# A hybrid encoder layer on eight cores: half of the transposes of the joint projection block moved to DMA, with shifts of loads, gate sums and one multiply

## The chip, the cores and the metric

The kernel runs as one program on all 8 cores of one Trainium2 chip. Each core works on its own rows, and no core talks to another. The metric is the device time in microseconds (us) of the slowest core. Engines are named as the profile names them: PE is TensorE (PEld its weight loads), DVE is VectorE, ACT is ScalarE, POOL is GpSimd, SP is SyncE, which here only issues DMAs.

## The reference, cut to what matters

One layer over sequences of 1024 channels:

```
h   = rmsnorm(x) * (1 + scale) + shift          # scale, shift, gate from silu(c) @ w_ada
z   = h @ w_in                                  # split: a, ga, u, v, gb, ma, mb
y_a = (real 2-D FFT of a, then a map per group) * silu(ga)
y_b = u * (w_s @ layernorm(v) + b_s) * silu(gb) # inside chunks of 128 positions
out = (sigmoid(ma) * (y_a @ w_pa) + sigmoid(mb) * (y_b @ w_pb)) @ w_out
y   = rmsnorm(x + gate * out) * final_g
```

Sizes: 16 prompts of 2048 positions and 4 samples of 4096 positions. Each core gets 6144 positions, as three units of 2048. The first unit is one sequence; the other two are either the two halves of a sample or two more prompts, and the kernel treats them together, as the "joint" pair.

## The kernel before, in words

Every engine runs one list of instructions in order, and so does the DMA queue of SP. The order is written out by hand: a class keeps, for each engine, the list and the semaphore waits that reads and writes of named 512-byte pieces of memory call for. A wait stands in front of its instruction, and all that is behind it on that engine waits too. All DMAs issued by SP go to one queue.

The work of a core falls in these stretches:

- The **first projection block** (an `ABlock` with f = 1, called `A`) computes the column section "a" of the first unit, chunk by chunk of 128 positions, does the first step of the FFT with one matmul (`stage1`), and writes the result to DRAM (`Gd`).
- Tiles 0 and 1 of 512 positions are done as a pair. `v_section`, `silu_section` and `u_section` are projections, with the second FFT step (`s3_single`) between them. `channel_tables` then builds tables from small inputs that `late_tabs` loads: cosines, biases, and, in the same group of DMAs and under the same semaphore, `final_g`. After it come `sgu`, `ga_section` with the last step of the FFT (`z_tr`, `fourier_gate`), then `merge_gates` and `merge` for eight blocks (`dmc`), and `out_chunk`.
- Tiles T = 2 and 3 run in the main loop. Beside their own work they sum up the gate vectors of the other units: `gate_load` brings rows of w_ada, `gate_acc` adds them on DVE.
- The **joint projection block** (`ABlock` with f = 0, called `A2`) comes after tile 3: 8 groups of 4 chunks for units 1 and 2. Chunks of x are loaded by SP into a ring of six slots. `sq` squares a pair of chunks on ACT, `rstd` makes 1/rms on POOL, `sc` scales the pair on DVE and then lets SP load into the freed slots. `fe` turns a group of four scaled chunks from positions by channels to channels by positions: 32 PE transposes into four PSUM banks, then eight moves out of PSUM that also apply scale and shift, four on DVE (line 473) and four on ACT (line 478). `a_proj` is 8 matmuls and a move on DVE (line 313); `stage1` is one matmul, a move, and a write to `Gd` (line 516). Group q + 1 is transposed between chunk 1 and chunk 2 of group q.
- Tiles 4 to 11 run in the main loop again. The input of tiles 3 and 5 to 11 is transposed by DMA (`dma_t`, line 439), and scale and shift are applied in place on DVE (`modulate`, line 445). At tiles 4 and 8 a new unit begins: w_out is loaded again by POOL's own DMA queue (`w_out_load`, line 689) and each of its eight rows of blocks is multiplied by the gate on POOL (`gate_mul`, line 694), between the additions that POOL does for `merge` (line 822).

`sgu` (line 755) makes four heads. For each head DVE writes one of two small buffers (line 761), and POOL multiplies it into the result (line 766). `fourier_gate` (lines 788 and 793, DVE) uses the memory of the first of these two buffers too, so it waits for POOL.

`out_chunk` (line 620) has two halves of 8 matmuls. With `split`, the first six of the first half are issued before the wait for the last blocks of the merge.

Of the kernel before, what the change touches and what calls it, by code (L numbers as in the profile page):

```python
# [11 lines left out]
D = 1024  # L12
# [198 lines left out]
def build_nc():  # L211
# [72 lines left out]
    semnames = (["pe", "act", "dve", "pool", "s_tab", "s_tb2", "s_id", "s_wst", "s_e", "s_gr", "s_gb", "s_wpa", "s_wpb", "s_wout"]  # L284
# [72 lines left out]

    def late_tabs():
# [7 lines left out]
        tab(fg_bc, dram_ap(final_g, 0, [[0, 128], [1, D]]))  # L366
        S.dma("sp", tabs, "s_tb2", writes=["tab2"] + ck)
# [74 lines left out]
    def modulate(off, slot):  # L442
        hT = hview(off)
        for kc in range(8):
# [8 lines left out]
    def fe_t(xoff):  # L453

        xr = bv(xoff, 4096).rearrange("p (j d) -> p j d", j=4)
        banks = []
        for kp in range(4):
# [8 lines left out]
    def fe_e(banks, off, slot):  # L466
        hT = hview(off)
        for kp, b in enumerate(banks):
            for kk in range(2):
                kc = 2 * kp + kk  # L470
                hk = gk(off + 1024 * kc, 1024)
                if kp % 2 == 0:
# [140 lines left out]
    def out_chunk(tb, T, j, k, split=False):  # L613
# [3 lines left out]
        xv = fv(XS[k], 1024)  # L617
        for half in range(2):
            b = newbank()
            mm = [lambda e, b=b, dmc=dmc, half=half: e.matmul(  # L620
                ps[b][:], lhsT=tb.mg[:, dmc, j * 128:(j + 1) * 128], rhs=w_out_sb[:, dmc, half * 512:(half + 1) * 512],
                start=(dmc == 0), stop=(dmc == 7)) for dmc in range(8)]
            cut = 6 if split and half == 0 else 0
            if cut:
                S.pe(mm[:cut], reads=gk(tb.m, 1024 * cut) + woutk, writes=[("ps", b)])
            S.pe(mm[cut:], reads=gk(tb.m, 8192) + woutk, writes=[("ps", b)])
# [10 lines left out]
        def fin():  # L637
            S.op("dve", lambda e: e.scalar_tensor_tensor(out=xv, in0=xv, scalar=stat[:, 1, si:si + 1], in1=fg_bc,
                                                         op0=ALU.mult, op1=ALU.mult),
                 reads=xk + [("st1", si), "tab2"], writes=xk)  # L640
# [111 lines left out]
    def sgu(tb):  # L752
        for h in range(4):
# [12 lines left out]
            S.op("pool", lambda e, h=h, ty=ty: e.tensor_tensor(out=tb.sgb[:, h, :], in0=ty, in1=tb.sgb[:, h, :], op=ALU.mult),  # L766
                 reads=gk(to, 1024) + sk, writes=sk)
# [58 lines left out]
    class ABlock:  # L826
# [3 lines left out]
        def __init__(self, f, nq, ring, N1, src, dst, xoffs, extra=()):  # L830
# [139 lines left out]
    pair = (T0, TB1)  # L970
    s3_begin(1)
# [3 lines left out]
    late_tabs()  # L975
# [11 lines left out]
    w_out_load()  # L987
    gate_load(0, 0)
# [54 lines left out]
    for T in range(2, NT):  # L1043
# [9 lines left out]
        def after(sec):  # L1053
# [7 lines left out]
            if T == 3 and sec < 3:  # L1061
                for kc, k in (((), ((0, 4), (1, 5), (2, 6)), ((3, 4), (4, 5), (5, 6)))[sec]):
                    gate_acc(2, kc, k, 7)
                for kc, k in ((((0, 4), (1, 5), (2, 6)), ((3, 4), (4, 5), (5, 6)), ((6, 4), (7, 5)))[sec]):
                    gate_load(kc, k)
                if sec == 2:
                    gate_bias(1, 6)
# [4 lines left out]
            if t == 0 and sec == 2:  # L1072
                gate_fetch(u)
                w_out_load()
# [3 lines left out]
        silu_section(tb, SEC["GB"], tb.sgb, tb.b, (lambda fc: s3j(fc - 1) if fc else None) if T == 4 else None)  # L1078
# [5 lines left out]
        sgu(tb)  # L1084
        ga_section(tb, u, t, (lambda fc: z_tr(0, fc)) if T == 4 else (lambda fc: z_tr(1, fc)) if T == 5 else None)
# [12 lines left out]
        for dmc in range(8):  # L1098
# [49 lines left out]
        elif isA:  # L1148
            A2.fe(0)
            A2.sq(3)  # L1150
# [6 lines left out]
        else:  # L1157
# [140 lines left out]
```

How the kernel before makes its waits and increments, by code:

```python
        def run(stream, e):  # L1176
            for it in stream:
                if it[0] == "wait":
                    e.wait_ge(sems[it[1]], it[2])
                elif it[0] == "raw":
                    it[1](e)
                else:
                    ins = it[1](e)
                    ins.then_inc(sems[it[2]], it[3])
```

## Time and profile before

| | us |
|---|---|
| runs | 1268.95, 1274.08, 1460.27 (median 1274.08) |
| profiled execution | 1266.18 |
| its span, slowest core (core 3) | 1264.6 |
| spans of all cores | 1256.6 to 1264.6 |
| PE busy | 1204.5 (95%) |
| DVE busy | 686.2 (54%) |
| ACT busy | 474.1 (37%) |
| POOL busy | 343.1 (27%) |
| mean DMA rate | 132 GB/s |

A row of a timeline gives the start and the length of a merged piece of work in us, the engine, the line of the kernel, the operation, the tiles, and the number of instructions. In square brackets stands the idle time of the engine before it and what ended it. SPq, POOLq and so on are the sequencers: a row SPq DMA_DIRECT2D is a DMA being issued, not moved. "DMA to landing" is the time from the issue until the data have landed. A window's row has the busy time and number of instructions of each engine, the granted clock of PE as a share of full speed, the busy share of the 16 DMA engines, and their rate.

### The profile page before, as it was taken

To read this page: it belongs to the slowest core of one execution; us is meant where nothing else is said; L and a number is where in the kernel's file an instruction comes from. 1 tells how busy PE (TensorE), PEld (TensorE's weight loads), DVE (VectorE), ACT (ScalarE), POOL (GpSimd) and SP (SyncE) were. 2 spreads that over 40 slices of the span, in tenths; PEclk is the share of its full clock that TensorE was granted. 3 is DMA by queue.
4 is the path that set the end of the run, shared out by engine and by line. 5 is a ranking of instruction groups with operands and counts; after the bars stand their busy time and mean duration, and the time that the engine had idled before them with its cause. 6 is when DMAs were issued, how large, how long until landed. Compare 5 with 4: busy or idle time off the path is not lost.

```text
span 1264.6 us, 19720 instructions; the slowest of 8 cores (1256.6 to 1264.6 us)
## 1 busy us (share of the span) xinstructions
PE 1204.5 (95%) x6128; PEld 563.5 (45%) x6128; DVE 686.2 (54%) x1109; ACT 474.1 (37%) x818; POOL 343.1 (27%) x430
## 2 busy tenths in 40 slices
PE   5799789999999899989999999999999999999997
PEld 1355444444444355545444444444444444444443
DVE  0483475465666568848356355545545654554444
ACT  1574232333323268835333332333242323332322
POOL 0231223631222232201811312313226323132211
PEclk9999899999999899999999999999999999999999
DMA  8999795334466278847230431513336415024121
GB/s 276 286 243 185 164 162 138 84 102 165 130 155 183 68 256 268 263 147 168 66 102 17 126 92 67 134 51 100 84 89 146 117 48 151 36 84 116 51 84 67
DMA packets 91124, 166.60 MB, mean 132 GB/s; under 512 B 39818, under 2 KB 52490, under 8 KB 89870
## 3 DMA queue, kind: packets, MB, share of 16 engines
q1 hardware_dynamic: 80606, 138.98, 36.9%
q0 software_dynamic: 9120, 17.96, 9.6%
q10 hardware_dynamic: 1296, 8.40, 2.0%
q8 instruction: 52, 0.85, 0.3%
q14 instruction: 50, 0.41, 0.1%
HBM read 143.41 MB, written 31.47 MB: 138 GB/s over the span
## 4 chain that ended last, share of the span: by engine, by line
PE 76%; DMA 7%; DVE 7%; issue 3%; POOL 2%; SPq 2%; ACT 1%; DVEq 0%; ACTq 0%; POOLq 0%
PE ps L699 35%; PE ps L620 12%; PE ps L503 6%; PE ps L811 6%; PE ps L817 6%; PE ps L709 5%; DMA arena<-w_ada 4%; PE ps L460 2%; POOL arena L766 2%; DVE arena L793 2%; DMA arena<-w_out 2%; DVE arena L788 1%; PE ps L924 1%; SPq L536 1%; DMA arena<-final_g 1%
## 5 line engine op out<-in xcount | busy, mean ns | idle before, releaser
L699 PE MATMUL ps<-arena 128*128 128x512 bf16 x2688 | 605.2, 381 | 3.7 <-DVE arena L761 2.4
L699 PEld LDWEIGHTS ps<-arena 128*128 128x128 bf16 x2688 | 262.8, 98 | 318.6 <-issue 10.9
L803 ACT ACTIVATE arena<-ps 128x512 bf16<-128x512 f32 x192 | 111.6, 595 | 244.1 <-PE ps L699 212.3
L822 POOL TENSOR_TENSOR arena<-arena 128x512 bf16<-128x512 bf16 x84 | 111.1, 1323 | 293.7 <-DVE arena L820 292.4
L620 PE MATMUL ps<-arena 128*128 128x512 bf16 x768 | 172.7, 379 | 4.4 <-DVE arena L822 3.0
L814 DVE TENSOR_TENSOR arena<-ps,arena 128x512 bf16<-128x512 f32 x96 | 66.2, 690 | 188.8 <-PE ps L811 182.9
L406 POOL TENSOR_TENSOR stat<-stat,eps_sb 128x1 f32<-128x1 f32 (+1 forms) x114 | 27.6, 242 | 396.4 <-ACT arena L632 291.7
L632 ACT ACTIVATE arena<-arena 128x1024 bf16<-128x1024 f32 x48 | 50.8, 1058 | 218.9 <-DVE arena L628 218.7
L419 ACT ACTIVATE arena<-arena 128x1024 bf16<-128x1024 f32 x96 | 101.4, 1056 | 73.8 <-DMA arena<-xB 54.0
L425 DVE TENSOR_SCALAR arena<-arena,stat 128x1024 bf16<-128x1024 f32 x96 | 84.5, 906 | 65.5 <-POOL stat L408 65.0
L620 PEld LDWEIGHTS ps<-arena 128*128 128x128 bf16 x768 | 74.2, 98 | 97.5 <-issue 10.1
L811 PE MATMUL ps<-arena 128*128 128x512 bf16 x384 | 99.4, 381 | 7.3 <-DVE arena L793 7.3
L313 DVE CAST arena<-ps 128x512 bf16<-128x512 f32 (+2 forms) x150 | 81.4, 583 | 43.3 <-ACT arena L311 19.2
L628 DVE TENSOR_TENSOR arena<-ps,arena 128x512 f32<-128x512 f32 x96 | 64.8, 688 | 71.1 <-PE ps L620 68.2
L817 PE MATMUL ps<-arena 128*128 128x512 bf16 x384 | 99.4, 382 | 0.0
L503 PE MATMUL ps<-arena 128*128 128x512 bf16 x384 | 91.8, 383 | 3.8 <-ACT arena L478 3.8
L709 PE MATMUL ps<-arena 128*128 128x512 bf16 x384 | 84.7, 379 | 0.0
L727 ACT ACTIVATE arena<-ps 128x512 bf16<-128x512 f32 x96 | 54.1, 600 | 64.7 <-PE ps L699 60.6
L408 POOL TENSOR_TENSOR stat<-stat,mh_sb 128x1 f32<-128x1 f32 (+1 forms) x114 | 71.2, 625 | 17.9 <-POOL stat L406 2.4
L820 DVE TENSOR_TENSOR arena<-ps,arena 128x512 bf16<-128x512 f32 x96 | 66.2, 690 | 15.0 <-PE ps L817 11.9
L720 ACT ACTIVATE arena<-ps,bnag 128x512 bf16<-128x512 f32 x48 | 33.4, 778 | 90.1 <-DVE bnag L716 90.1
L311 ACT ACTIVATE arena<-ps 128x352 bf16<-128x352 f32 (+3 forms) x103 | 44.9, 488 | 54.2 <-PE ps L924 15.8
(75 smaller groups left out, 942.2 us busy)
## 6 DMA issues: line engine op xcount, KB each, us to landing
arena<-xB SPq DMA_DIRECT2D x96, 512.0 KB, 5.2
arena<-xA SPq DMA_DIRECT2D x48, 512.0 KB, 6.3
yu<-arena SPq DMA_DIRECT2D x48, 512.0 KB, 2.8
arena<-w_ada SPq DMA_DIRECT2D x24, 512.0 KB, 6.0
arena<-w_in POOLq DMA_DIRECT2D x9, 1024.0 KB, 17.6
arena<-w_ada ACTq DMA_DIRECT2D x8, 1024.0 KB, 24.0
Gd<-arena SPq DMA_DIRECT2D x48, 128.0 KB, 4.7
arena<-Gd SPq DMA_DIRECT2D x12, 512.0 KB, 9.4
```

Source lines behind the costliest of these rows:

```text
L313: S.op("dve", lambda e: e.tensor_copy(out=dst, in_=src), reads=reads, writes=writes)
L408: S.op("pool", lambda e: e.tensor_tensor(out=dst, in0=dst, in1=mh_sb[:, 0:n], op=ALU.pow), reads=wk + ["mh"], writes=wk)
L419: S.op("act", lambda e: e.activation(out=junk, in_=fv(XS[k], 1024), func=AF.Square, scale=0.03125, accum_out=stat[:, 0, si:si + 1]), reads ...
L425: S.op("dve", lambda e: e.tensor_scalar(out=xr, in0=fv(XS[k], 1024), scalar1=stat[:, 1, si:si + 1], scalar2=None, op0=ALU.mult), reads=gk( ...
L503: S.pe([lambda e, kc=kc: e.matmul(ps[b][:], lhsT=hT[:, kc, j * 128:(j + 1) * 128], rhs=w_in_sb[:, 0, kc, :], start=(kc == 0), stop=(kc == ...
L620: mm = [lambda e, b=b, dmc=dmc, half=half: e.matmul(ps[b][:], lhsT=tb.mg[:, dmc, j * 128:(j + 1) * 128], rhs=w_out_sb[:, dmc, half * 512:( ...
L699: S.pe([lambda e, kc=kc: e.matmul(ps[b][:], lhsT=w_in_sb[:, sec, kc, col:col + 128], rhs=tb.hT[:, kc, :], start=(kc == 0), stop=(kc == 7)) ...
L709: S.pe([lambda e, kc=kc, b=b, j=j: e.matmul(ps[b][:], lhsT=tb.hT[:, kc, j * 128:(j + 1) * 128], rhs=w_in_sb[:, SEC["V"], kc, :], start=(kc ...
L803: S.op("act", lambda e, b=b, so=so: e.activation(out=bv(so, 512), in_=ps[b][:], func=AF.Sigmoid), reads=[("ps", b)], writes=gk(so, 1024))
L811: S.pe([lambda e, k=k: e.matmul(ps[b][:], lhsT=w_pa_sb[:, k, dmc * 128:(dmc + 1) * 128], rhs=tb.sga[:, k, :], start=(k == 0), stop=(k == 3 ...
L817: S.pe([lambda e, k=k: e.matmul(ps[b2][:], lhsT=w_pb_sb[:, k, dmc * 128:(dmc + 1) * 128], rhs=tb.sgb[:, k, :], start=(k == 0), stop=(k == ...
L822: S.op("pool" if dmc < 7 else "dve", lambda e: e.tensor_tensor(out=tb.mg[:, dmc, :], in0=tb.mg[:, dmc, :], in1=bv(sl[1], 512), op=ALU.add) ...
```

## The change

1. In the joint block (`half=True`, only for `A2`) `fe` transposes the lower four channel blocks on PE, into two banks, and all four moves out of PSUM are on ACT. The upper four blocks are transposed by four DMAs of SP (one per chunk, 128 by 512 elements, `fe_dma`) and modulated in place by four DVE instructions (`fe_mod`). `fe_dma(q + 1)` stands at the start of group q, `fe_mod(q + 1)` where `fe(q + 1)` stands. For group 0, `fe_dma(0)` is issued in tile 3's last merge step, after `sc(2)`.
2. `late_tabs` is issued before `s3_begin(1)`, and `final_g` is loaded apart from it, later, under its own semaphore.
3. `sgu`: the multiply of heads 1 and 3 goes from POOL to DVE.
4. `out_chunk` with `split`: the first six matmuls of both halves come before the wait.
5. Tile 3's `gate_acc` and `gate_load` calls are spread over its gb section and the first two merge steps; two loads are issued at the end of tile 2.
6. `gate_fetch` and `w_out_load` of tiles 4 and 8 come after `sgu` instead of before it.

```diff
@@ class ABlock
         def fe(self, g):
-            fe2(self.dst[g][0], self.dst[g][1], self.xoffs[g % 2])
+            if not self.half:
+                fe2(self.dst[g][0], self.dst[g][1], self.xoffs[g % 2])
+                return
+            off, slot = self.dst[g]
+            fe_e(fe_t(self.xoffs[g % 2], 2), off, slot, True)
+
+        def fe_dma(self, g):
+            if self.half:
+                off = self.dst[g][0]
+                xr = bv(self.xoffs[g % 2], 4096).rearrange("p (j d) -> p j d", j=4)
+                for j in range(4):
+                    S.dma("sp", [lambda e, j=j: e.dma_start_transpose(out=hview(off)[:, 4:8, j * 128:(j + 1) * 128], in_=xr[:, j, 512:1024])],
+                          "s_tr%d" % j, reads=gk(self.xoffs[g % 2] + 2048 * j, 2048),
+                          writes=[("hraw", off, j)] + (gk(off + 4096, 4096) if j == 0 else []))
+
+        def fe_mod(self, g):
+            if self.half:
+                modulate(self.dst[g][0], self.dst[g][1], range(4, 8))
         def body(self, hooks):
             for q in range(self.nq):
+                self.fe_dma(q + 1)
                 for j in range(4):
                     if j == 2:
                         self.fe(q + 1)
+                        self.fe_mod(q + 1)
@@ tile 3, merge loop and its end
                 if dmc in (3, 5, 7):
                     A2.sc(dmc // 2 - 1)
+                if dmc == 7:
+                    A2.fe_dma(0)
...
             A2.fe(0)
+            A2.fe_mod(0)
             A2.sq(3)
             out_chunk(tb, T, 0, OS[0])
@@ def sgu
-            S.op("pool", lambda e, h=h, ty=ty: e.tensor_tensor(...),
-                 reads=gk(to, 1024) + sk, writes=sk)
+            S.op(("pool", "dve")[h % 2], lambda e, h=h, ty=ty: e.tensor_tensor(...),
+                 reads=gk(to, 1024) + sk, writes=sk + (gk(to, 1024) if h % 2 else []))
@@ def out_chunk
+        nf = 6 if split else 0
+        for half in range(2 if split else 0):
+            S.pe(mm[half][:nf], reads=gk(tb.m, 1024 * nf) + woutk, writes=[("ps", bs[half])])
         for half in range(2):
-            ...
+            S.pe(mm[half][nf:], reads=gk(tb.m, 8192) + woutk, writes=[("ps", b)])
@@ tiles 0 and 1
+    late_tabs()
     s3_begin(1)
     A.fe(5)
     for tb in pair:
         v_section(tb)
-    late_tabs()
...
     w_out_load()
+    final_tab()
@@ tile 3's gate sums
-            if T == 3 and sec < 3:
-                ... (3 gate_acc after the gb section, 3 after u, 2 at dmc 0)
+            if T == 3 and sec == 0:
+                gate_load(2, 6)
+                gate_acc(2, 0, 4, 7)
+                gate_load(3, 4)
+            if T == 3:                      # inside the gb section, fc = 0..3
+                k = (5, 6, 4, 5)[fc]
+                gate_acc(2, fc + 1, k, 7)
+                if fc + 4 < 8:
+                    gate_load(fc + 4, k)    # the last three at dmc 0 and 1
@@ main loop
         sgu(tb)
+        if t == 0:
+            gate_fetch(u)
+            w_out_load()
```

## Rows read from the trace of the kernel before

**Rows 1.** What PE waited for, whole span: in total, times, longest
```profile
PE ps L811 <- DVE arena L793: 7.3, 7, 3.8
PE ps L777 <- DVE arena L761: 6.3, 6, 1.9
PE ps L381 <- DMA arena<-final_g: 6.1, 1, 6.1
PE ps L620 <- DVE arena L822: 3.0, 9, 0.6
```
**Rows 2.** Timeline of PE, around the channel tables
```profile
140.71 0.77 PE L381 MATMUL ps<-arena 128*128 128x128 f32 x2 [6.09 <-DMA arena<-final_g]
```
**Rows 3.** Timeline of SP's DMA issues, same stretch
```profile
105.95 12.39 SPq L536 DMA_DIRECT2D arena<-Gd  x4
```
**Rows 4.** Windows of 4 us, same stretch
```profile
108.00:112.00 4.00, 4.00 (x20) 1.85 (x19) 2.02 (x6) 1.42 (x3) 0.09 (x1) 1.00 1.00 127
140.00:144.00 4.00, 3.29 (x15) 3.32 (x16) 0.43 (x1) 1.06 (x3) 0.00 (x0) 0.50 0.19 77
```
**Rows 5.** Timeline of PE, tile 3's first merge steps
```profile
419.40 1.87 PE L811 MATMUL ps<-arena 128*128 128x512 bf16 x4 [3.84 <-DVE arena L793]
422.77 4.81 PE L699 MATMUL ps<-arena 128*128 128x512 bf16 x16
427.42 1.03 PE L811 MATMUL ps<-arena 128*128 128x512 bf16 x4
429.14 3.62 PE L699 MATMUL ps<-arena 128*128 128x512 bf16 x16
```
**Rows 6.** Timeline of DVE: tile 3 before sgu, tile 6 in sgu
```profile
402.64 4.05 DVE L659 SCALAR_TENSOR_TENSOR arena<-arena,cs_sb 128x1024 f32<-128x1024 f32 x3
770.74 0.75 DVE L761 SCALAR_TENSOR_TENSOR arena<-ps,lng_sb,arena 128x512 bf16<-128x512 f32 x1 [2.22 <-POOL arena L766]
774.07 0.76 DVE L788 TENSOR_TENSOR arena<-arena 128x256 f32<-128x256 bf16 x2 [1.47 <-POOL arena L766]
```
**Rows 7.** Timeline of POOL, tile 8
```profile
939.03 1.58 POOL L689 DMA_DIRECT2D arena<-w_out  x2
959.40 4.24 POOL L694 TENSOR_TENSOR arena<-arena 128x1024 bf16<-128x1024 bf16 x2 [14.29 <-DMA arena<-w_out]
988.40 1.16 POOL L822 TENSOR_TENSOR arena<-arena 128x512 bf16<-128x512 bf16 x1 [0.33 <-DVE arena L820]
```
**Rows 8.** Timeline of PE, joint block
```profile
458.49 1.95 PE L460 MATMUL ps<-arena 128*128 128x128 bf16 x32
460.27 7.07 PE L620 MATMUL ps<-arena 128*128 128x512 bf16 x32
479.98 1.89 PE L503 MATMUL ps<-arena 128*128 128x512 bf16 x8
515.98 1.95 PE L460 MATMUL ps<-arena 128*128 128x128 bf16 x32
525.54 1.95 PE L460 MATMUL ps<-arena 128*128 128x128 bf16 x32
```
**Rows 9.** Windows, joint block
```profile
506.00:516.00 10.00, 10.00 (x72) 5.52 (x71) 9.10 (x16) 7.72 (x14) 2.24 (x4) 1.00 0.97 306
470.00:474.00 4.00, 4.00 (x44) 2.82 (x43) 3.82 (x7) 1.92 (x3) 1.34 (x2) 1.00 1.03 379
```
**Rows 10.** Line 401 (x loads), issues between 461.3 and 463 us: issue, landing
```profile
L401 SPq DMA_DIRECT2D arena<-xA x2: 328/354/381, 461.0 to 461.7; - x2
DMA to landing us min/median/max: 11.4/11.4/11.4
```
**Rows 11.** Line 439 (DMA transposes of 128x1024), whole span: issue ns, landing
```profile
L439 SPq DMA_TRANSPOSE arena<-arena x32: 1222/1224/2869, 343.1 to 1152.7; - x32
DMA to landing us min/median/max: 3.0/3.1/5.1
```
**Rows 12.** Line 445 (modulate in place), whole span: ns min/median/max
```profile
L445 DVE TENSOR_SCALAR arena<-arena,Gtab,modT x64: 404/406/415, 367.6 to 1161.5; 128x512 bf16<-128x512 bf16 x64
```

More of the change, by code:

```diff
@@ L356, in build_nc, with final_tab @@
     S.dma("sp", tabs[:1], "s_tab", writes=["tabs"])
+    def final_tab():
+        S.dma("sp", [lambda e: e.dma_start(out=fg_bc, in_=dram_ap(final_g, 0, [[0, 128], [1, D]]))], "s_tb3", writes=["fg"])
     def late_tabs():
@@ L440, in dma_t, with modulate @@
               "s_tr%d" % j, reads=gk(O_XSR + 2048 * jr, 2048), writes=[("hraw", off, j)] + (gk(off, 8192) if j == 0 else []))
-    def modulate(off, slot):
+    def modulate(off, slot, kcs=range(8)):
         hT = hview(off)
-        for kc in range(8):
+        for kc in kcs:
             S.op("dve", lambda e, kc=kc: e.tensor_scalar(
@@ L451, in hview, with fe_t @@
         return bv(off, 4096).rearrange("p (k n) -> p k n", k=8)
-    def fe_t(xoff):
+    def fe_t(xoff, n=4):
         xr = bv(xoff, 4096).rearrange("p (j d) -> p j d", j=4)
         banks = []
-        for kp in range(4):
+        for kp in range(n):
             b = newbank()
@@ L471, in fe_e @@
                 hk = gk(off + 1024 * kc, 1024)
-                if kp % 2 == 0:
+                if kp % 2 == 0 and not act:
                     S.op("dve", lambda e, b=b, kk=kk, kc=kc: e.tensor_scalar(
@@ L617, in out_chunk @@
         xv = fv(XS[k], 1024)
-        for half in range(2):
[L619 to L626, printed above, removed]
+        bs = [newbank() for _ in range(2)]
+        mm = [[lambda e, b=bs[half], dmc=dmc, half=half: e.matmul(
+            ps[b][:], lhsT=tb.mg[:, dmc, j * 128:(j + 1) * 128], rhs=w_out_sb[:, dmc, half * 512:(half + 1) * 512],
+            start=(dmc == 0), stop=(dmc == 7)) for dmc in range(8)] for half in range(2)]
+        nf = 6 if split else 0
+        for half in range(2 if split else 0):
+            S.pe(mm[half][:nf], reads=gk(tb.m, 1024 * nf) + woutk, writes=[("ps", bs[half])])
+        for half in range(2):
+            b = bs[half]
+            S.pe(mm[half][nf:], reads=gk(tb.m, 8192) + woutk, writes=[("ps", b)])
             hk = gk(XS[k] + 2048 * half, 2048)
@@ L639, in fin @@
                                                          op0=ALU.mult, op1=ALU.mult),
-                 reads=xk + [("st1", si), "tab2"], writes=xk)
+                 reads=xk + [("st1", si), "fg"], writes=xk)
             tok = S.dma("sp", [lambda e: e.dma_start(out=yu.ap()[row0:row0 + 128, :], in_=xv)],
@@ L765, in sgu @@
                 reads=[("ps", b), "Ktab", "tab2"], writes=gk(to, 1024))
-            S.op("pool", lambda e, h=h, ty=ty: e.tensor_tensor(out=tb.sgb[:, h, :], in0=ty, in1=tb.sgb[:, h, :], op=ALU.mult),
-                 reads=gk(to, 1024) + sk, writes=sk)
+            S.op(("pool", "dve")[h % 2], lambda e, h=h, ty=ty: e.tensor_tensor(out=tb.sgb[:, h, :], in0=ty, in1=tb.sgb[:, h, :], op=ALU.mult),
+                 reads=gk(to, 1024) + sk, writes=sk + (gk(to, 1024) if h % 2 else []))
     def z_tr(uz, g):
@@ L826, in build_nc, with __init__ @@
     class ABlock:
-        def __init__(self, f, nq, ring, N1, src, dst, xoffs, extra=()):
+        def __init__(self, f, nq, ring, N1, src, dst, xoffs, extra=(), half=False):
+            self.half = half
             self.f, self.nq, self.ring, self.N1, self.src, self.dst = f, nq, ring, N1, src, dst
@@ L1071, in after, with in_gb @@
                 gate_load(sec, 6)
-            if t == 0 and sec == 2:
-                gate_fetch(u)
-                w_out_load()
         v_section(tb)
         after(0)
-        silu_section(tb, SEC["GB"], tb.sgb, tb.b, (lambda fc: s3j(fc - 1) if fc else None) if T == 4 else None)
+        def in_gb(fc):
+            if T == 4 and fc:
+                s3j(fc - 1)
+            if T == 3:
[3 more added lines that the diff above has]
+                    gate_load(fc + 4, k)
+        silu_section(tb, SEC["GB"], tb.sgb, tb.b, in_gb)
         after(1)
@@ L1093, in build_nc @@
                         [(hoffs[g % 2], 1 + g // 4) for g in range(8)] + [(O_HT, 1)], (O_XSR, XS[10]),
-                        extra=[("z", g, 1) for g in range(4)])
+                        extra=[("z", g, 1) for g in range(4)], half=True)
             A2.load_to(2)
@@ L1111, in build_nc @@
             if T == 3 and dmc == 0:
+                gate_acc(2, 5, 6, 7)
                 gate_acc(2, 6, 4, 7)
+                gate_bias(1, 6)
+            if T == 3 and dmc == 1:
                 gate_acc(2, 7, 5, 7)
@@ L1165, in build_nc @@
                 gate_store(1, 6)
+                gate_load(0, 4)
+                gate_load(1, 5)
             out_chunk(tb, T, 1, OS[1])
```

11 lines of the change are left out of this document (2 added, 9 removed).

## Prediction

> **What bounds the kernel now.** PE does: 95% of the span is PE busy. So I read first PE's list of waits [rows 1]: 7.3 us before L811 (the first merge of a tile, late because DVE's fourier gate is late), 6.3 us before L777, 6.1 us before the channel tables, 3.0 us before an out chunk. Those are what parts 2 to 6 of the change can win. Then the joint block. There PE is at 100% in every window, but it is not alone: DMA is at 0.97 of its time at 306 GB/s [rows 9]. The reader is to see both limits lie side by side: a group of four chunks takes PE 9.56 us (from one set of PE transposes to the next, 515.98 to 525.54) [rows 8]. In that time SP's queue moves four loads of 0.524 MB and four writes of 0.131 MB, 2.62 MB, or 8.6 us at 306 GB/s. About one microsecond is free. Last, how deep the queue is where the block begins: a load issued at 461.0 or 461.7 landed 11.4 us later [rows 10].
>
> **Channel tables.** PE idled 6.1 us for final_g [rows 1, 2], which now comes later; the other tables are issued before the Gd loads. At 140 to 144 us the granted clock was 0.50, the 1.2 GHz level [rows 4]; with no idle ahead of it the 16 small fp32 matmuls there should take half their 3.9 us: 1.9 us. Against it: the tables, 0.9 MB, now stand ahead of the Gd loads in a DMA that is 100% busy [rows 4], at a time when four Gd issues took 12.39 us [rows 3]. 0.9 MB at 306 GB/s is 3 us, and I charge all of it to PE. Bounds: 0 (the Gd loads wait for their data anyway) and 6 (half the rate). Sum: -6.1 - 1.9 + 3.0 = **-5.0**.
>
> **sgu.** At tile 6 DVE waits 2.22 us for POOL's first one, and the fourier gate 1.47 us for the last [rows 6]. With heads 1 and 3 on DVE, the gate starts after POOL's second multiply, some 1.2 us earlier, for two DVE instructions more (0.4 us each, by the in-place one [rows 12]). The waits before L811, apart from 3.84 at tile 3 and 1.84 at tile 8, are 7.3 - 5.68 = 1.6 us, each below 0.6: all go. **-1.6**. Of L777's 6.3 us most is at tiles 0 and 1, where eight heads run at POOL's pace; they will run at DVE's (two of L761 at 0.75 and one multiply of 0.4, 1.9 us for two heads, where POOL sets 2.2): -1.4 there, and -1.4 at tiles 4 and 5. **-2.8**. Bounds -1 and -6.
>
> **Tile 3.** The wait of 3.84 us before L811 [rows 5] ends with the fourier gate. Three gate sums (4.05 us) stand on DVE just ahead of sgu [rows 6]; they go into the gb section, and sgu gives 1.2 more. The wait goes. With it goes the low clock behind it: L811 took 1.87 against 1.03, L817 as much, L699 4.81 against 3.62 [rows 5], together 2.9. **-6.7**. What is late next: nothing, the gate ends some 1.5 us before the merge. Bounds -3.8 and -6.7.
>
> **out_chunk.** Six more matmuls (6 x 0.216 = 1.3 us) stand before the wait, which is 0.25 to 0.6: the waits go, except tile 8's, below. **-2.5**.
>
> **w_out behind sgu.** POOL now does two multiplies, the second behind DVE, before it issues w_out at tile 8: 3.2 us later than 939.03 [rows 7]. From the landing at 959.40 to 989.56 POOL works without a gap but for 0.33 us [rows 7]: gate multiplies, merge additions and rstd. So this chain sets when the out chunk can begin, and it ends 3.2 us later. The 1.84 us that PE waited before L811 at tile 8 are no gain, they are waited for later. Less the out chunk's own wait of 0.45: **+2.8**. Bounds 0 and +5 (a low clock behind the wait). At tile 4 the issue is 5 us later, but POOL has 4.1 us of gaps in the chain and 3.7 behind it: 0.
>
> These parts together: -5.0 - 1.6 - 2.8 - 6.7 - 2.5 + 2.8 = **-15.8**.
>
> **Joint block: what is saved.** 16 of 32 PE transposes per group; 32 take 1.79 us (458.49 to 460.27) [rows 8], so 0.9 us each for nine groups, 8.1 us. ACT has four moves as before. DVE has four in-place modulates (0.41 each [rows 12]) for four moves out of PSUM, about the same. Added on SP: four issues per group, at most 1.22 us each [rows 11], 4.9 us beside 2.6 of loads and writes: under 8.7, SP is not the bound.
>
> **What the four transposes cost in DMA.** No row shows one of 128x512. The whole one needs 3.1 us from issue to landing, of which 1.22 is the issue [rows 11]: 1.9, so 0.95 for a half, 3.8 for four as upper end. Lower end: 0.524 MB at the best rate seen, 379 GB/s [rows 9], 1.4. I take 3.0, nearer to the row of the same instruction. The Trainium skill (DMA: Bandwidth & Descriptors, "Latency and other measured facts") gives 261 GB/s for such a transpose: an estimate from it is 2.0 us for four, and the three loaded groups below would each be 1 us shorter. The trace has no rate for a transpose alone, so this stays apart.
>
> **Group 0.** fe_dma(0) stands on SP behind the two loads that sc(2) frees, the last issued at 461.7. That one lands at 461.7 + 11.4 = 473.1 [rows 10]. The transposes are behind it in the same queue: 473.1 + 3.0 = 476.1, modulate 1.4, so 477.5. PE has two out chunks to do and is free at 460.27 - 0.9 + 6.9 = 466.3 [rows 8]: it idles 11 us. DVE stands in fe_mod(0) all that time, and behind it are both out chunks' additions, sc(3) and the first moves of a_proj. sc(3) frees two ring slots, so loads come 14 us later too. Worked forward: DVE ends out chunk 0, sc(3) and out chunk 1 at 482, group 1's transposes (behind sc(3)'s loads, issued at 480) land at 488.5, group 0's last move ends at 490.8, and group 1 starts at 494.2 instead of 479.98 [rows 8]: **+14.2**, in which the savings of two sets are included.
>
> The Trainium skill (same page, "Queues, rings and completion order") says that each DMA engine takes a queue's descriptors in ring order; by that rule the transposes cannot pass the loads. The 11.4 us of [rows 10] at 0.97 busy agree.
>
> **Groups 1 to 7.** After an out chunk (groups 1 and 2) the queue has time to drain and the transposes land about 6 us into the group, just in time: 0.5 and 0.6 us won. Groups 3 to 5: DVE's second sc ends 1.5 us into the group, its two loads (3.5 us at 300 GB/s) are ahead of the transposes, then 3.0, then about 1 to land: 9.0 us. From there to the next group are modulate 1.4, a move 0.6 and stage1 with its wait 0.7: 11.7 us instead of 9.56, +2.1 each, **+6.3**. By the ends 1.4 and 3.8 it is +0.5 and +2.9 each. Groups 6 and 7 have no loads: -0.7 each. Block: 14.2 - 1.1 + 6.3 - 1.3 = **+18.1**.
>
> **Sum.** 1266.18 - 15.8 + 18.1 = 1268.5. That is against the profiled execution; the median of the runs shown, 1274.08, is 8 above it.
>
> **Rivals.**
> - **Only the start is late** (chance 0.22). If small packets fit into what looks busy, groups 1 to 7 each win 0.9: 14.2 - 6.3 = +7.9, 1258.3. For it: 379 GB/s in one window [rows 9], against a mean of about 300. Against it: 0.97 busy.
> - **The transposes are hidden** (0.13). The queue is less deep at 462 us than now, or they land before PE's out chunks end: -8.1, 1242.3. For it: 3.1 us to landing elsewhere [rows 11]. Against it: 11.4 us.
> - **The clock falls in the new gaps** (0.17); the slower side. After 3.84 us of idle, work at 1.2 GHz cost 2.9 us [rows 5]. Gaps of 11 us, two in group 0 and three of about 3 us: five times 2.9 is 14.5, 1283. [...] Against it: in groups that wait for DMA slower matmuls only fill the wait.
> - The forecast: 0.44. Other cases, such as a Gd load that PE waits for at tiles 0 and 1 longer than charged: 0.04.
>
> That a part does nothing is excluded by the code: each moves instructions.
>
> **Numbers.** Predicted 1268. The range takes in the forecast with its bounds (the transposes' price +-4, the tables +-3, sgu +-3, tile 8 +-3), the rivals at 1258 and 1283, and stops above the hidden case: 1249 to 1287. A measurement of this kernel tells 2% (25 us) from no change. Faster needs 1241: half of the hidden case, 0.06. Slower needs 1291: the clock rival with every bound against it, 0.04. Within 2%: 0.90.
>
> **What would show it.** In the changed kernel's trace: PE idle of about 11 us before the first L503 of the joint block, waiting for DVE's modulate, and DVE idle of like length before it for arena<-arena; a transpose there that needs over 10 us to land; sets of PE transposes at 0.9 us each, 11 to 12 us apart in groups 3 to 5 and near 8.7 in groups 6 and 7. The wait for final_g and the 3.84 at tile 3 are gone; POOL issues w_out at tile 8 behind two multiplies, and PE waits some 6 us in tile 8's merges or before its out chunk. It is wrong if the first a_proj follows the out chunks within 2 us, or if groups 3 to 5 are under 9.2 us.

## The result, and the profile after

The changed kernel takes **1295.13 us** (median of 4 runs, 1293.23 to 1296.91); on the same chip the kernel before took 1266.17, 1268.95 and 1274.08 us. The ratio on record is 1.0231, 95% interval 1.0213 to 1.0249, so **2.3% slower**; the quotient of the two medians is a little less, 1.0206. Times and ratios here and below are of runs in the fast state; in the slower one, in which the cores of a die show a lower granted clock, the kernel before also took 1460.27 us. The prediction was 1268, range 1249 to 1287. The profiled execution took 1293.99 us; its slowest core is core 6 (1292.2 us). Core 3, on which the prediction's rows lie, has 1286.4 us, and is shown unless another is named.

The span and the share of each engine, first of core 6, then (last line) of core 3:

```profile
span 1292.2 us, 19399 instructions; the slowest of 8 cores (1279.8 to 1292.2 us)
PE 1198.9 (93%) x5869; PEld 557.7 (43%) x5984; DVE 698.8 (54%) x1133; ACT 474.5 (37%) x818; POOL 319.1 (25%) x406
PE 1207.5 (94%) x5984; PEld 558.2 (43%) x5984; DVE 699.9 (54%) x1133; ACT 475.0 (37%) x818; POOL 316.2 (25%) x406
```

The change takes 144 PE transposes away: 6128 matmuls before, 5984 on core 3. Core 6 shows only 5869, so 115 records are missing there and its busy time is no measure. On core 3 PE is busy 3.0 us *more* than before (1207.5 for 1204.5), although the 144 transposes were worth about 8 us: so the other matmuls took some 11 us longer (an estimate from these), at a lower granted clock (0.976 on the mean, 0.989 before). The span of this core is 21.8 us longer, so 18.8 of them are idle time. PE's list of waits (who, for whom, total us, times, longest), beside [rows 1]:

```profile
PE ps L515 <- DVE arena L313: 24.8, 13, 4.5
PE ps L575 <- DMA arena<-Gd: 6.7, 1, 6.7
PE ps L505 <- DVE arena L447: 6.5, 1, 6.5
```

The wait for final_g is gone, those before the merge (L811, now L814) and the out chunk (L620, now L621) nearly so. In their place PE waits for the FFT's data at tiles 0 and 1, and, most of all, in the joint block for moves out of PSUM on DVE (L313). DVE in turn waits for the transposes: 39.5 us in nine waits, by the view of their line (issue ns, landing in us), which answers to [rows 11]:

```profile
L887 SPq DMA_TRANSPOSE arena<-arena x36: 1173/1266/3009, 454.5 to 568.8; - x36
  DVE arena L447: 39.5, 9
DMA to landing us min/median/max: 2.4/4.1/8.6
```

**The joint block by groups.** A group starts with the a_proj of its chunk 0 in PE's timeline. Lengths in us, of core 3:

| | before | after | more | forecast |
|---|---|---|---|---|
| first PE transposes to start of group 1 | 21.5 | 30.9 | +9.4 | +14.2 |
| group 1 | 13.0 | 18.3 | +5.3 | -0.5 |
| group 2 | 9.6 | 10.8 | +1.2 | -0.6 |
| group 3 | 9.6 | 14.1 | +4.5 | +2.1 |
| group 4 | 9.6 | 12.9 | +3.4 | +2.1 |
| group 5 | 9.6 | 13.1 | +3.6 | +2.1 |
| groups 6 and 7, to tile 4 | 20.3 | 24.2 | +3.9 | -1.3 |
| block | 93.0 | 124.2 | +31.2 | +18.1 |

Core 6 has 93.0 and 121.5; the mean of the eight cores is 93.0 and 122.3. The start was better than forecast, all the rest worse. The start first: SP's issues, DVE and PE (start and length in us).

```profile
453.39 0.99 SPq L403 DMA_DIRECT2D arena<-xA  x2
454.52 7.86 SPq L887 DMA_TRANSPOSE arena<-arena  x4
```
```profile
464.74 1.38 DVE L447 TENSOR_SCALAR arena<-arena,Gtab,modT 128x512 bf16<-128x512 bf16 x4 [10.77 <-DMA arena<-arena]
```
```profile
450.84 1.06 PE L462 MATMUL ps<-arena 128*128 128x128 bf16 x16
466.26 6.03 PE L505 MATMUL ps<-arena 128*128 128x512 bf16 x16 [6.54 <-DVE arena L447]
472.35 1.06 PE L462 MATMUL ps<-arena 128*128 128x128 bf16 x16
```

The wait that was forecast is there, DVE idle for 10.77 us and PE for 6.5 instead of 11: the transposes are issued right behind two loads, and the last of them has landed 10.2 us after the first was issued. The two loads ahead landed 8.5 us after their issue, at about 462, and all four transposes after them, at 463.1 to 464.7. Now the groups behind it, SP and DVE (a part):

```profile
514.68 6.28 SPq L887 DMA_TRANSPOSE arena<-arena  x4
525.65 1.00 SPq L403 DMA_DIRECT2D arena<-xA  x2
526.74 0.37 SPq L518 DMA_DIRECT2D Gd<-arena  x1
527.27 6.20 SPq L887 DMA_TRANSPOSE arena<-arena  x4
```
```profile
522.33 1.38 DVE L447 TENSOR_SCALAR arena<-arena,Gtab,modT 128x512 bf16<-128x512 bf16 x4 [5.13 <-DMA arena<-arena]
523.62 1.28 DVE L313 CAST arena<-ps 128x512 bf16<-128x512 f32 x2
524.82 1.41 DVE L427 TENSOR_SCALAR arena<-arena,stat 128x1024 bf16<-128x1024 f32 x2
535.42 1.38 DVE L447 TENSOR_SCALAR arena<-arena,Gtab,modT 128x512 bf16<-128x512 bf16 x4 [3.58 <-DMA arena<-arena]
```

This is a closed loop over two engines that each work in order. SP issues four transposes from 514.68, and they are landed at 522.33, 7.65 us later. DVE modulates (1.4), makes the two moves that stood behind (1.3), and scales the next pair (1.4, to 526.2). That frees two ring slots; SP issues their loads and a write, and only then the next four, at 527.27: 12.6 us per turn. (The scale also writes the data that these four read, so they could not go before it in any queue.) The next turns are 13.1 and 12.0. PE, waiting in it, also loses its clock:

```profile
524.45 0.58 PE L515 MATMUL ps<-arena 128*128 128x512 bf16 x1 [4.54 <-DVE arena L313]
524.83 3.62 PE L505 MATMUL ps<-arena 128*128 128x512 bf16 x8
```
```profile
524.00:526.00 2.00, 1.55 (x4) 0.65 (x5) 2.00 (x4) 0.60 (x1) 0.00 (x0) 0.50 0.98 342
```

Behind 4.54 us of idle the granted clock (the third number from the end) is 0.50, the 1.2 GHz level, and eight matmuls take 3.62 us, where they take 1.89 at 1.00 [rows 8].

The DMA engines are as full in this longer group as in the group of 9.56 us before, at a lower rate (share and GB/s are the last two numbers; before: 0.97 and 306 [rows 9]). So this trace alone does not tell whether the loop of waits or the work of the DMA engines sets its length; `ghost` and `ghostwait` below take them apart.

```profile
527.00:540.00 13.00, 10.72 (x56) 4.87 (x54) 7.79 (x15) 8.74 (x17) 1.78 (x4) 0.91 0.96 248
```

**Tiles 0 and 1.** From tile 0's to tile 2's first matmul: 182.3 us before, 183.5 after (core 6: 178.8 and 188.9). SP and PE:

```profile
96.06 0.70 SPq L338 DMA_DIRECT2D arena<-cosC  x1
104.41 22.23 SPq L538 DMA_DIRECT2D arena<-Gd  x4
```
```profile
130.86 1.86 PE L575 MATMUL ps<-arena 128*128 128x128 bf16 x16 [6.70 <-DMA arena<-Gd]
143.66 0.39 PE L385 MATMUL ps<-arena 128*128 128x128 f32 x2
```

The small fp32 matmuls of the tables are at full clock (0.39 a pair against 0.63), as forecast; but the four Gd issues hold SP for 22.23 us instead of 12.39 [rows 3], and PE waits 6.70 us for what they bring (5.2 to 11.3 us on the eight cores). And the low clock comes behind this wait instead: L575 takes 1.86 us for 1.06 and the 16 matmuls of L702 behind it 5.55 for 3.62.

**Tile 3, tile 8.** PE in tile 3's first merge steps, beside [rows 5], and POOL at tile 8, beside [rows 7]:

```profile
414.59 1.03 PE L814 MATMUL ps<-arena 128*128 128x512 bf16 x4
415.45 1.03 PE L820 MATMUL ps<-arena 128*128 128x512 bf16 x4
416.32 3.62 PE L702 MATMUL ps<-arena 128*128 128x512 bf16 x16
```
```profile
965.51 1.59 POOL L692 DMA_DIRECT2D arena<-w_out  x2
984.55 4.23 POOL L697 TENSOR_TENSOR arena<-arena 128x1024 bf16<-128x1024 bf16 x2 [17.45 <-DMA arena<-w_out]
```

Tile 3's wait and the low clock behind it are gone; the stage from its first matmul to the joint block is 6.8 us shorter on core 3, where it was the longest of all cores (85.4 us), and 4.1 on the mean of the eight (83.4 to 79.4). At tile 8 POOL issues w_out behind its multiplies, and from the landing on works without a gap; the tile is 1.6 us longer (core 6: 3.6).

### The profile page after: what moved, and what is told of

Same layout as the page of the kernel before. It is cut to its first block, busy times and chain, and to the rows that moved or that the text cites. A ratio compares the mean times of both kernels' runs of the same rounds, so it can differ in the third digit from the quotient of the medians.

```text
span 1292.2 us, 19399 instructions; the slowest of 8 cores (1279.8 to 1292.2 us)
## 1 busy us (share of the span) xinstructions
PE 1198.9 (93%) x5869; PEld 557.7 (43%) x5984; DVE 698.8 (54%) x1133; ACT 474.5 (37%) x818; POOL 319.1 (25%) x406
## 4 chain that ended last, share of the span: by engine, by line
PE 72%; DMA 11%; DVE 6%; SPq 3%; issue 3%; POOL 2%; ACT 1%; ACTq 0%; DVEq 0%; POOLq 0%
PE ps L702 39%; PE ps L621 11%; PE ps L820 5%; PE ps L814 5%; PE ps L712 5%; DMA arena<-w_ada 4%; SPq L887 3%; PE ps L505 2%; DMA arena<-Gd 2%; DMA arena<-arena 2%; DMA arena<-xA 1%; DVE arena L313 1%; DVE arena L427 1%; DMA arena<-xB 1%; PE ps L462 1%
## 5 line engine op out<-in xcount | busy, mean ns | idle before, releaser
L702 PE MATMUL ps<-arena 128*128 128x512 bf16 x2616 | 602.5, 382 | 11.0 <-ACT arena L806 4.9
L702 PEld LDWEIGHTS ps<-arena 128*128 128x128 bf16 x2688 | 263.0, 98 | 323.7 <-issue 19.3
L621 PE MATMUL ps<-arena 128*128 128x512 bf16 x757 | 172.2, 382 | 1.9 <-DVE arena L825 0.8
L817 DVE TENSOR_TENSOR arena<-ps,arena 128x512 bf16<-128x512 f32 x96 | 66.2, 690 | 184.0 <-PE ps L814 180.4
L427 DVE TENSOR_SCALAR arena<-arena,stat 128x1024 bf16<-128x1024 f32 x96 | 87.5, 938 | 72.7 <-POOL stat L410 69.9
L621 PEld LDWEIGHTS ps<-arena 128*128 128x128 bf16 x768 | 75.3, 98 | 93.4 <-issue 5.1
L313 DVE CAST arena<-ps 128x512 bf16<-128x512 f32 (+2 forms) x150 | 81.5, 583 | 46.5 <-ACT arena L311 31.8
L814 PE MATMUL ps<-arena 128*128 128x512 bf16 x375 | 96.8, 379 | 2.0 <-DVE arena L796 1.5
## 6 DMA issues: line engine op xcount, KB each, us to landing
arena<-w_ada ACTq DMA_DIRECT2D x8, 1024.0 KB, 24.2
```

What stands on the lines that cost most here:

```text
L313: S.op("dve", lambda e: e.tensor_copy(out=dst, in_=src), reads=reads, writes=writes)
L427: S.op("dve", lambda e: e.tensor_scalar(out=xr, in0=fv(XS[k], 1024), scalar1=stat[:, 1, si:si + 1], scalar2=None, op0=ALU.mult), reads=gk( ...
L621: mm = [[lambda e, b=bs[half], dmc=dmc, half=half: e.matmul(ps[b][:], lhsT=tb.mg[:, dmc, j * 128:(j + 1) * 128], rhs=w_out_sb[:, dmc, half ...
L702: S.pe([lambda e, kc=kc: e.matmul(ps[b][:], lhsT=w_in_sb[:, sec, kc, col:col + 128], rhs=tb.hT[:, kc, :], start=(kc == 0), stop=(kc == 7)) ...
L814: S.pe([lambda e, k=k: e.matmul(ps[b][:], lhsT=w_pa_sb[:, k, dmc * 128:(dmc + 1) * 128], rhs=tb.sga[:, k, :], start=(k == 0), stop=(k == 3 ...
```

## Experiments

Ratios are those on record, to the kernel before on the same chip, with 95% intervals; the quotient of two medians can differ from them by some tenths of a per cent. "Block" is the joint block of cores 3 and 6, 93.0 and 93.0 before.

### Which part costs: the joint block alone, and all the others alone

```diff
-  extra=[("z", g, 1) for g in range(4)], half=True)
+  extra=[("z", g, 1) for g in range(4)], half=False)    # others; joint is the reverse: before + part 1
```

> The changed kernel with the joint block's transposes all on PE as before; parts 2 to 6 stay. Theory 1 (the loss sits in the joint block, +31 us on core 3, and the other parts give back about 9): 1263 us, ratio to before 0.993. Theory 2 (the reordered table loads, up to 10 us on core 6, eat what the other parts win on the slowest core): 1268 to 1272. The forecast had 1254 for this (1270 - 15.8).

> The kernel before with the joint block's DMA transposes alone. Theory 1: the joint block costs about 31 us by itself, 1301 us. Theory 2 (it costs more only because the other parts bring tile 3's end earlier, ahead of the loads): under 1293. The forecast had +18: 1288.

Others: 1261.89 us, 0.9990 (0.9976 to 1.0004). Joint: 1295.21 us, 1.0273 (1.0228 to 1.0318), block 125.2 and 123.3. So part 1 of the change has the whole loss, and parts 2 to 6, forecast at 15.8 us, gain about one: between 3.0 and nothing, by the interval.

### Tables back to their place, final_g still apart

```diff
@@ others
-    late_tabs()
     s3_begin(1)
...
     for tb in pair:
         v_section(tb)
+    late_tabs()
```

> As others, but the small tables' loads stand where they stood before (behind the Gd loads), final_g still apart. Theory 1 (the tables ahead of the Gd loads delay those; only final_g was worth moving): 6 us less than others on the slowest core, 1257 us, the wait for arena<-Gd of 7 to 11 us gone and no wait for final_g. Theory 2 (the Gd loads are late whatever is ahead of them): within 2 us of others.

1253.84 us, 0.9930 (0.9904 to 0.9956). The issue of the four Gd loads is 9.87 us again, PE's wait for Gd is gone, and tiles 0 and 1 take 173.9 us (others: 185.3).

```profile
106.82 9.87 SPq L538 DMA_DIRECT2D arena<-Gd  x4
```

The term "tables" was two edits. The small tables ahead of the Gd loads cost 8 us of the median (11 on core 3, 8.2 on the mean of the eight cores' tiles 0 and 1). What taking final_g apart gives is not shown, as no run changes it alone: in `joint`, which has the tables as before, PE waits 1.7 to 4.8 us for final_g, by core (3.5 to 6.1 in the trace of before), and in `tabs`, at the same place, up to 3.6 us for b_s, the load just ahead of it.

### The start: group 0's transposes ahead of sc(2)'s loads

```diff
+  if dmc == 7:
+      A2.fe_dma(0)
   if dmc in (3, 5, 7):
       A2.sc(dmc // 2 - 1)
-  if dmc == 7:
-      A2.fe_dma(0)
```

> The changed kernel with group 0's transposes issued ahead of the two loads that sc(2) frees, instead of behind them. Theory 1 (the queue is served in order): they land some 4 us earlier, PE's wait of 6.5 us before the first a_proj shrinks to 1 to 3, 1290 us. Theory 2 (the wait is for the transposes' own time): 1295.

1289.72 us, 1.0211 (1.0197 to 1.0226); block 120.8 and 120.5. PE's wait before the first a_proj falls from 6.5 to 2.9 us, as by theory 1; the block is 3.4 and 1.0 us shorter. The start is not where most of the time is.

### The wait moved: modulate after chunk 3 instead of before chunk 2

```diff
   self.fe(q + 1)
-  self.fe_mod(q + 1)
...
+  self.fe_mod(q + 1)      # after the loop over j; two sets of semaphores
   if q in hooks:
```

> The changed kernel with the modulate of group q+1 moved on DVE from between chunks 1 and 2 to behind chunk 3 of group q (semaphores of the transposes doubled for it). Theory 1 (a loop through SP and DVE: four issues 6.2 us, landing 1.4, modulate 1.3, moves and sc 2.6, then the loads on SP: 12.6 us a group): the loads no longer wait behind the modulate, the loop is cut, groups take 9.5 to 10.5 us and the kernel about 1280. Theory 2 (the 16 DMA engines are full, so the place of the modulate does not matter): 1293 to 1297.

1290.82 us, 1.0222 (1.0188 to 1.0256); block 120.0 and 118.1. PE's waits:

```profile
PE ps L505 <- DVE arena L447: 22.7, 6, 6.6
PE ps L515 <- DVE arena L313: 5.7, 3, 3.5
```

Both theories missed. The block is 4.2 and 3.4 us shorter, but what DVE's moves no longer wait for, PE's next group waits for itself: for the most part only the place of the wait changed. The transposes are late even for the last moment at which they are needed.

### What makes a transpose dear: number, size, loads beside it

`two`: the same bytes per group by two DMAs of 128x1024 (chunks 2 and 3). `quarter`: half the bytes, still four DMAs. `one`: half the bytes in one DMA (chunk 3). `thin`: the x loads of the block bring only 512 of 1024 columns, so part of x is left out.

```diff
# two (one: j = 3 alone)
-  for j in range(4):
-      ... out=hview(off)[:, 4:8, j * 128:(j + 1) * 128], in_=xr[:, j, 512:1024]
+  for j in (2, 3):
+      ... out=hview(off)[:, :, j * 128:(j + 1) * 128], in_=xr[:, j, :]
# quarter
+      ... out=hview(off)[:, 6:8, j * 128:(j + 1) * 128], in_=xr[:, j, 768:1024]
# thin
+  ... e.dma_start(out=fv(XS[k], 1024)[:, 0:512], in_=self.src(i)[:, 0:512])
```

> The changed kernel with the same bytes transposed by DMA in another cut: chunks 2 and 3 of each group whole, by two DMAs of 128x1024, chunks 0 and 1 whole on PE (eight half-width moves on ACT, eight half-width modulates on DVE). Theory 1 (SP's issue time, about 1.3 to 1.5 us each whatever the size, sets the group's length): two issues fewer, 3 us a group, the kernel 1272 to 1278. Theory 2 (DMA bytes set it): 1293 to 1297.

> The changed kernel with half the bytes: four DMAs of 128x256 for the top two channel blocks, the other six on PE (two of their moves on DVE). Theory 1 (issue time): four issues as before, SP still needs 5 to 6 us for them, the kernel 1290 to 1296. Theory 2 (bytes): half of the joint block's loss goes, 1278 to 1284.

> The changed kernel with chunk 3 alone transposed by DMA, whole, by one DMA of 128x1024 per group; three chunks on PE, their moves shared by ACT and DVE. The bytes are those of quarter (1284 us), the issues one instead of four. If bytes alone count: 1282 to 1286. If SP's issue time is a second limit close beneath the drain, so that both must fall: 1272 to 1278.

> The changed kernel where each x load of the joint block but the first two brings only the first 512 of 1024 columns (its output is wrong for it). The earlier runs showed 1295 us with the same bytes in two issues and 1284 with half the bytes in four. Theory 3 (the transposes drain behind the two loads issued just ahead of them, and DVE and the next loads wait for that): 1.7 us less ahead of each group's transposes and a queue that is never full, PE's wait before group 0 falls from 6.5 to about 2, groups take 10 to 11 us, the kernel 1272 to 1278. Theory 1 (four issues at about 1.27 us on SP set the pace): 1 us less a group, 1287 to 1290.

| | time | ratio (95%) | block |
|---|---|---|---|
| two | 1294.79 | 1.0252 (1.0234 to 1.0269) | 120.6, 124.0 |
| quarter | 1284.38 | 1.0171 (1.0156 to 1.0185) | 113.4, 114.5 |
| one | 1292.65 | 1.0237 (1.0209 to 1.0264) | 124.8, 124.9 |
| thin | 1284.33, 1282.63 | 1.0165 (1.0130 to 1.0200) | 115.5, 111.9 |

SP in `two`, with loads ahead in the queue and, in the last row, without:

```profile
537.67 5.15 SPq L900 DMA_TRANSPOSE arena<-arena  x2
549.43 2.61 SPq L900 DMA_TRANSPOSE arena<-arena  x2
```

and the line of `quarter`, and DVE's wait in `one`:

```profile
L889 SPq DMA_TRANSPOSE arena<-arena x36: 1152/1212/2627, 458.7 to 562.8; - x36
```
```profile
DVE arena L899 <- DMA arena<-arena: 22.4, 7, 9.5
```

`two` came out by its theory 2, `quarter` at the upper edge of it; for `one` and `thin` both theories missed (`thin` has two runs to go by). A transpose is issued in about 1.2 us whether it is 128x256, 128x512 or 128x1024, when nothing is ahead of it (the shortest took 1.15, 1.17 and 1.22). My theory that the number of issues sets the price fell all the same: two issues behind loads take 5.15 us where four take 6.2. So SP is held back by what is in its queue as well. Half the loads' bytes or half the transposes' bytes give back a quarter to a third of the block's excess each. `one` can't be read for the price: its moves out of PSUM share 512-byte pieces with the transpose and so wait for it too, and DVE has eight smaller modulates.

### The loads on another queue

```diff
-  x_load(self.ring[i % nr], self.src(i), self.extra if i < nr else (), after)
+  x_load(..., after, "pool" if self.half else "sp")
```

> The changed kernel with the x loads of the joint block issued from POOL's DMA queue instead of SP's (semaphores of the transposes doubled for it). Theory 3 in its narrow form (it is the order in one queue that holds the transposes back): they pass the loads, PE's wait before the first a_proj goes from 6.5 to 0 to 3, the kernel 1280 to 1286. In its wide form (the 16 engines are shared, and their total work sets the pace): 1290 to 1297.

1314.84 and 1309.06 us, slower than both theories; ratio 1.0390 (1.0327 to 1.0453), block 129.5 and 128.2. The time from the first to the second set of PE transposes fell from 21.5 to 13.7 us, two of the later ones rose (from 18.3 to 22.8 and from 15.7 to 20.6). SP and DVE in the latter:

```profile
514.77 6.75 SPq L887 DMA_TRANSPOSE arena<-arena  x4
527.76 1.38 DVE L447 TENSOR_SCALAR arena<-arena,Gtab,modT 128x512 bf16<-128x512 bf16 x4 [10.43 <-DMA arena<-arena]
```

The x loads are not what is late: ACT waits 0.6 us for them in the whole block. The transposes are. With no load ahead of them in their queue, DVE's modulate begins 12.8, 8.9, 13.0, 10.0 and 13.2 us after their first issue in groups 1 to 5; in the changed kernel it is 9.1, 9.6, 7.7, 8.2 and 8.0. So in these groups it is not the order in one queue that holds them back. The Trainium skill (DMA: Bandwidth & Descriptors, "Issuing engines are not separate DMA queues") says that spreading DMAs over issuing engines brings no bandwidth, only issue time; this run agrees, as the transposes came no sooner by it but in one group (8.9 us for 9.6).

### The DMA work without the wait, and both on top of PE's transposes

`ghost`: all transposes on PE as before; the same four DMAs per group in groups 3 to 8, into spare memory. `ghostwait`: with one DVE instruction per group that waits for them. `halflate`: the real change, in groups 3 to 8 alone.

```diff
# ghost, ghostwait (fe_dma)
-  out=hview(off)[:, 4:8, j * 128:(j + 1) * 128], in_=xr[:, j, 512:1024]
+  out=spare[:, :, j * 128:(j + 1) * 128], in_=xr[:, j, 512:1024]
# halflate, in fe, fe_dma and fe_mod
-  if self.half:
+  if self.half and g > 2:
```

> The edits outside the joint block (as 'others'), the joint block with all 32 PE transposes per group, and beside them, in groups 3 to 8, the same four transposes of 128x512 from the same x, issued by SP at the same place, but into spare memory that nobody reads (one DVE instruction waits for them once, at the end). The result is unchanged. Theory 'the wait' (DVE stands in order in front of the modulation while the transposes land): nobody waits here but SP's queue, so 1262 to 1266, groups of 9.6 us. Theory 'the queue' (SP's issue time and the 16 DMA engines, whose share rose from 0.70 to 0.96, push the x loads behind PE): the loads come late here as well, 1275 to 1283, groups 3 to 7 over 11 us, with PE waiting at the end on x loads through ACT's squares and DVE's scales.

> As 'ghost', with one DVE instruction on the spare memory in each of the groups 3 to 8, at the place of the modulation, that waits for the four transposes. Theory 'the wait': most of what the half transposes of these six groups cost comes back, 1275 to 1285, with ghost at 1262 to 1266. Theory 'the queue': within 4 us of ghost.

> The changed kernel, with the half transposes by DMA in groups 3 to 8 alone; groups 0 to 2 are all on PE. It gives what six groups cost when they replace PE work, and takes the start away. Of the 32.6 us of the joint edits, the first three groups' intervals hold 14 (21.5, 13.2, 18.3 against 12.4, 13.0, 13.0), so 1277 to 1282 if the rest stays; if the start's delay alone feeds the later groups, 1265 to 1270.

| | time | ratio (95%) | block |
|---|---|---|---|
| others | 1261.89 | 0.9990 (0.9976 to 1.0004) | 93.2, 93.2 |
| ghost | 1266.26, 1268.16 | none | 100.2, 98.3 |
| ghostwait | 1275.56 | 1.0077 (1.0048 to 1.0107) | 105.1, 106.2 |
| halflate | 1276.10 | 1.0089 (1.0066 to 1.0113) | 107.5, 109.6 |

(Others ran in another session, beside 1263.06 for the kernel before. Ghost has two runs to go by, too few for a ratio; the kernel before took 1263.2 to 1267.4 us beside them.) Both theories hold a share, on core 3 then core 6. The DMA work alone makes the block 7.0 and 5.1 us longer: in one group ACT waits 4.88 us for x in front of its square, and the moves behind it on ACT, DVE's next scale and PE come late by it.

```profile
517.44 1.06 ACT L421 ACTIVATE arena<-arena 128x1024 bf16<-128x1024 f32 x1 [4.88 <-DMA arena<-xA]
```

One waiting instruction on DVE adds 4.9 and 7.9. The rest, 2.4 and 3.4, comes with the real thing, although PE then has fewer transposes: the first chunks wait for them in fact. Ghost's timeline of SP shows the issues as long as in the changed kernel:

```profile
516.16 6.24 SPq L887 DMA_TRANSPOSE arena<-arena  x4
527.40 6.31 SPq L887 DMA_TRANSPOSE arena<-arena  x4
```

and DVE's wait in ghostwait:

```profile
515.82 0.41 DVE L894 TENSOR_SCALAR arena<-arena,Gtab,modT 128x512 bf16<-128x512 bf16 x1 [5.28 <-DMA arena<-arena]
```

Six groups cost 14.5 and 16.5 us, 2.4 to 2.8 each, with no late start ahead of them. The other 16.7 and 11.9 us of the changed kernel's block come with the start and the groups it upsets.

### The version that the experiments point to

```diff
@@ tabs (no DMA transposes, tables in their old place, final_g apart)
-        sgu(tb)
         if t == 0:
             gate_fetch(u)
             w_out_load()
+        sgu(tb)
```

> No DMA transposes in the joint block, the small tables loaded where they were, final_g apart, and gate_fetch and w_out_load back ahead of sgu; sgu on two engines, the split out chunk and the spread gate sums stay. The run with w_out behind sgu gave 1254.4. Theory (w_out's landing sets POOL's chain in tile 8): tile 8 gets 1.5 us shorter, 1253 us. Rival (its issue on POOL ahead of the first multiply delays the gate as much): 1254 to 1255.

1252.63 us, 0.9913 (0.9882 to 0.9943): 0.9% faster than the kernel before, which is clear of the noise though under 2%. Against `tabs` (0.9930) the step of w_out is not resolved.

## Why the prediction was wrong

**The step that failed is "Groups 1 to 7"**: +3.9 us forecast for them, +21.9 measured. Three of its parts:

1. *The transposes in a loaded group.* From the end of DVE's second scale to the landing I put 7.5 us: 3.5 for the data of two loads, 3.0 for the transposes' DMA time, 1 to land. Measured, 526.2 to 535.42, are 9.2. "SP is not the bound" compared a sum of issues with a group's length; but these issues lie in series on the loop. From 526.2 SP needs 1.0 us to finish the loads and the write, 6.2 for four transposes, not 4.9 at most, and the last lands 2.0 later. A turn is 12.0 to 13.1 instead of 11.7. The 4.9 came from reading 1.22 as the most that an issue takes; [rows 11] has it as the median, and 2.87 as the longest. The clearest case is a group without loads, which I had put at -0.7: in group 7 four transposes are issued from 563.80 in 6.21 us, and DVE's modulate begins at 571.37, after 4.33 us of waiting and 7.6 after the first issue.
   By the Trainium skill (DMA: Bandwidth & Descriptors, "Latency and other measured facts"), four such transposes at 261 GB/s would be 2.0 us; the issues alone, 5.1 to 7.9 us here, hide what the rate is, so no run here shows it.
2. *"Just in time" in group 1.* DVE waited 5.37 us for the transposes there too, where I had given the queue time to drain after an out chunk. The four were issued from 483.36 on in 6.24 us, and DVE's modulate began at 492.47, 9.1 us after the first issue, longer than in the steady groups. Behind the gap the out chunk ran at the 1.2 GHz level in part (5.30 us for 3.62).
3. *The clock, which I had made a rival.* In groups 4 and 6 the first chunks ran at the 1.2 GHz level: 3.62 for 1.89 us. It is part of the +3.4 and +3.9. In all, PE's matmuls took some 11 us longer by it, near the rival's 14.5, but how much of this lengthens the span, and how much only fills waits, was not tested apart.

The mechanism was right in part: DVE stands in order before the modulation, and ghostwait against ghost shows this at 4.9 and 7.9 us for six groups. Ghost shows a second share of like size, 7.0 and 5.1 us, that I had not priced: x loads that come late by the added DMA work, though nobody waits for the transposes.

**The start.** +9.4 us of +14.2; PE idle 6.5, not 11. The queue was less deep than 11.4 us [rows 10]: the two loads ahead landed in 8.5, and the last of four transposes 10.2 us after the *first* issue. The 11.4 of [rows 10] told how deep the queue was, not that nothing passes in it; that these transposes landed behind the loads is seen only in the changed kernel's trace. The rival "only the start is late" is excluded.

**Channel tables.** This step failed too: -5.0 forecast; measured on core 3 for tiles 0 and 1, with sgu's share, is +1.2 in the changed kernel and +3.0 in `others`. The gains of 6.1 and 1.9 came. But PE's new wait is 6.7 (core 6: 11.3), beyond my upper bound of 6, and behind it comes a low clock of its own that I had no term for: from the first L575 to the second PE needs 7.3 us, and needed 4.6. -6.1 - 1.9 + 6.7 + 2.7 is +1.4, near the +1.2 measured. I had charged 0.9 MB at 306 GB/s, a rate of another stage; in that stretch DMA moved 127 GB/s while 100% busy [rows 4], and by that row it is 7.1 us. That is one window of 4 us: its neighbours from 96 to 128 us moved 172 to 229.

The gain of 6.1 was also priced from the core that waited longest: the other seven waited 3.5 to 4.9 us for final_g. On the mean of the eight cores tiles 0 and 1 take 180.0 us before, 184.9 after, 184.0 in `others`, and 175.8 in `tabs`; but 177.3 in `joint`, whose code is there that of before, so 3 us of such a difference can be scatter between executions.

**Tile 3**: -6.7 forecast, -6.8 measured on core 3, but -4.1 on the mean of the eight cores. The agreement is that of the core whose rows I had read, and which had the longest such stage. **out_chunk**: its waits are gone but for 1.2 us. **sgu**: tiles 6 and 7 are 1.2 and 0.8 us shorter, out chunks included. In tiles 0 and 1 nothing of it is left on core 3: from the end of the table matmuls to the first merge PE takes 40.9 us before and 41.0 after. **w_out behind sgu**: counted from the start of tile 8, w_out is issued 3.5 us later (3.2 forecast) and landed 2.2 later; the tile is +1.6 on core 3, +3.6 on core 6 (forecast +2.8 less what other parts save there).

Sum, with the shares as measured: the joint block missed by 13.1 us, and parts 2 to 6 by some 14.5 of the slowest core's time (-15.8 forecast, -1.3 by the ratio of `others`; the mean of its eight cores' spans is 5.3 us shorter). The larger part of both misses is of one kind, the price of more work put into a DMA queue that was already full. The rest of the second is that waits read on one core of one execution were summed as gains of the slowest core.

## What to carry to other kernels

When DMA shows 0.97 busy beside a PE at 100%, moving work from PE to DMA takes it to where almost nothing is free; ask what a turn of the loop through the queue and the in-order engine that waits for it costs, issue times in series. Price extra bytes by the rate of the very stretch they go into. Read a wait on all cores before summing it as a gain. And take a bundle of edits apart: here the tables, moved along with `final_g`, cost 8 us that the bundle hid.

## What was not expected of the hardware

- The issue of a DMA transpose takes about 1.2 us of SP at 128x256 (median 1.21, shortest 1.15), 128x512 (1.27, 1.17) and 128x1024 (1.22, 1.22 [rows 11]): it hardly shrinks with the size. A plain load is issued in 0.35 us [rows 10].
- In `two`, behind loads in the same queue, two issues take 5.15 us; without loads ahead, 2.61.
- Four Gd issues took 9.87 us (`tabs`) and 12.39 us (before) with the tables behind them, and 22.23 us with the tables just ahead. That a long issue on SP tells of a full queue is argued from these, not shown by itself.
- Taking the loads off SP's queue did not bring the transposes sooner: 8.9 to 13.2 us from their first issue to DVE's modulate in groups 1 to 5 of `poolq`, for 7.7 to 9.6.
